# Index scores moved between the products of two projection panels, the key norm taken sooner, and two of four token tiles scaled by ScalarE before their transposition

## The chip, the cores and the metric

The kernel runs on one NeuronCore of a Trainium2 chip, as one launch. The metric is device time in microseconds. Before the change it was 1379.87 us, the median of three runs (1375.46 to 1380.01).

## What is computed

Two transformer blocks over 512 tokens of width 1024, in fp32. The first has windowed attention with sinks beside differential attention, then a feed-forward part with a short convolution. The second, `hybrid_layer`, has sparse latent attention whose keys are chosen by an index, beside a recurrent branch. The parts that the change touches:

```python
def rms_norm(x, g):        # also at the ends of the first block's two halves
    xf = xf * lax.rsqrt(jnp.mean(xf * xf, axis=-1, keepdims=True) + EPS)
    return (xf * g.astype(jnp.float32)).astype(x.dtype)
...
        x = x + rms_norm(jnp.einsum("bse,ed->bsd", mix, w_out[layer]), attn_post_g[layer])
        h2 = rms_norm(x, ffn_pre_g[layer])
        f = conv_ffn(h2, w_up[layer], conv_w[layer], conv_b[layer], w_down[layer])
        x = x + rms_norm(f, ffn_post_g[layer])
...
    z = xn @ w_in
    q, c_kv, q_idx, k_idx, w_idx, g_attn, x_rnn, g_rnn, merge = split_cols(z)
    c_kv = rms_norm_2(c_kv, kv_norm_g)
    k_idx = layer_norm(k_idx, idx_ln_g, idx_ln_b)
...
        s_idx = jax.nn.relu(jnp.einsum('btjd,bsd->btjs', qi.astype(f32), k_idx_f))
        s_idx = jnp.einsum('btjs,btj->bts', s_idx, wi.astype(f32))
        s_idx = jnp.where(causal[None], s_idx, -jnp.inf)
        _, idx = lax.top_k(s_idx, topk)
```

There are 8 index heads of width 64, and each query keeps 128 keys.

## The kernel before

**Products.** An fp32 product is made of three fp32r products, of a rounded high part and a low rest: high by high, high by low, low by high. Weights come as 100 panels of 256 columns by 1024 rows, loaded by SyncE's queue into two raw buffers. ScalarE makes the high part (`hi`, L850), VectorE (`lo`, L1296) or GpSimd (L332) the low part; each feeds the panel two further on. `one_panel` (L339) multiplies a panel: 16 passes, each of three matmuls of 512 columns, the first 8 passes for the first half of the panel's columns, the others for the second. It starts once its low part stands (`w_lo`) and the panel two before it has been copied out of PSUM (`evac`). PG holds the two panels in work, PX the side products.

**Token-wise norms, n2 and n4.** The last two panels of the stages out1 and dn3 leave their result with tokens on the partitions, in four tiles t of 128 tokens (Y4 and F4). Per tile, VectorE adds the last half (L1537, L1663), ScalarE squares it with a sum (`half_squares`, L891) and takes a root (L906), and VectorE makes 1 over the root with one Newton step and a diagonal matrix DG from it (`token_factor`, L1520 to L1525). TensorE multiplies each 128x128 piece of the tile with DG (L440), which scales and transposes at once: `turn_all` runs the chunks 0 to 5, the tiles 0 and 1 first, then tile 2, then tile 3; `turn_rest` the chunks 6 and 7 inside the next panel. VectorE then updates the residual (L1549) and ScalarE and VectorE split it (L923, L1554) for the first panel of the next stage, up0 or in2a. VectorE does tile t wholly before it adds tile t+1.

**Norms n3 and n5.** The sum of squares over the 1024 rows is one product with a constant matrix in `mean_square` (L390), two fp32 matmuls, issued between panel 0 and panel 1 of up0 and of in2a. They wait until VectorE has added the squares (L1273). From the sum ScalarE makes R by a logarithm and an exponential, and no panel of the stage is copied out before R stands.

**in2a and the index.** in2a has seven panels: 0 the latent and the index key, 1 and 2 the index queries QI, 3 to 6 the attention queries. Side products (the index weights w_idx, the means and sums of the latent and the key) stand after panels 1 to 4. ScalarE and VectorE split the queries and the normed key into high and low (QIH, QIL, KIH, KIL), the last of these after panel 6. Then, between in2a and the next stage xr, a loop of 24 units runs alone: unit u is head u % 8 of query block u // 8 + 1, three fp32r matmuls with 64 rows and n = 256, 384 or 512 columns (L725 to L727), into one of four PG banks. ScalarE takes the positive part (L1125, two buffers RLU), VectorE adds it times the head's weight into MD (L1726). Unit u waits for ScalarE's unit u-4, ScalarE's unit u for VectorE's unit u-2, and xr for ScalarE's last.

**Top-k.** 16 rounds of `topk_round` (L1741, L1744) on VectorE follow: 3, 2, 1 and 2 in the four panels of xr, 1 at the end of rg, 3, 2 and 2 in wr. The result is needed only after wr.

## Time and profile before

| | |
|---|---|
| time, median of three | 1379.87 us |
| the profiled execution's own time | 1380.44 us |
| its span, first to last instruction | 1378.3 us |
| busy: PE, VectorE, ScalarE, GpSimd | 96%, 62%, 42%, 16% of the span |
| mean granted TensorE clock | 0.983 of 2.4 GHz |

PE is TensorE's matmuls, which are pipelined: the time that one takes from the next is the distance between two starts, not the duration in the row. A wait is idle time of an engine just ahead of an instruction, with the instruction whose end closed it. The rows below come from one execution, so sums are made against 1380.44 us.

### The profile page before, as it was taken

The page shows a single profiled execution, that of the slowest core. Times are in us where ns is not written, and L with a number is a line of the kernel's source. Part 1 is how long each engine was busy: PE and PEld are TensorE (multiplying, and loading weights), DVE is VectorE, ACT ScalarE, POOL GpSimd, SP SyncE. Part 2 cuts the span into 40 slices and gives each one's busy share as a digit, 9 for nine tenths or more (in the row PEclk, how much of TensorE's full clock was granted, in tenths as well). Part 3 has the DMA queues.
Part 4 walks back from the last instruction along what each step waited for, and adds up shares of the span by engine and source line. Part 5 has one row for each costly group of instructions (what it writes and reads, how often), then busy time and mean ns, then how long its engine had stood idle before and what let it go on. Part 6 is the DMA issues. An engine that isn't in the chain of part 4 may idle for free.

```text
span 1378.3 us, 16092 instructions
## 1 busy us (share of the span) xinstructions
PE 1316.8 (96%) x5982; PEld 1032.8 (75%) x5982; DVE 854.3 (62%) x1497; ACT 579.6 (42%) x872; POOL 219.7 (16%) x173
## 2 busy tenths in 40 slices
PE   7999988899999999999999999999999989999996
PEld 6777656688888888888888867777778856658885
DVE  6455753798888378738863532568887656663342
ACT  5344645634443134324322444323673246653321
POOL 1322211000000000000000023420005411114450
PEclk9999998999999999999999999899999999999999
DMA  5211100132222223222232131402122210002411
GB/s 193 92 62 61 62 31 31 61 107 106 92 91 91 95 104 107 92 92 92 91 111 103 62 146 69 153 31 92 62 96 92 101 49 31 32 31 92 153 62 61
DMA packets 17788, 116.52 MB, mean 85 GB/s; under 512 B 1984, under 2 KB 2240, under 8 KB 4544
## 3 DMA queue, kind: packets, MB, share of 16 engines
q1 hardware_dynamic: 16320, 108.35, 22.2%
q10 hardware_dynamic: 1408, 7.37, 1.4%
q8 instruction: 38, 0.62, 0.2%
q14 instruction: 22, 0.18, 0.0%
HBM read 111.52 MB, written 4.19 MB: 84 GB/s over the span
## 4 chain that ended last, share of the span: by engine, by line
PE 85%; DVE 10%; ACT 3%; issue 1%; DMA 1%; DVEq 0%; ACTq 0%; SPq 0%
PE PG L352 17%; PE PG L354 17%; PE PG L353 17%; PE PX L494 5%; PE PX L763 3%; PE PX L430 2%; PE PX L428 2%; PE PX L429 2%; PE PG L430 2%; PE PG L428 2%; PE PG L429 2%; PE PG L792 2%; PE PX L671 1%; PE PX L802 1%; DVE MD L1726 1%
## 5 line engine op out<-in xcount | busy, mean ns | idle before, releaser
L352 PE MATMUL PG<-XH,WH 128*128 128x512 f32 x992 | 392.2, 395 | 5.9 <-DVE XL L1554 2.7
L332 POOL TENSOR_TENSOR WL<-RAW,WH 128x512 fp32r<-128x512 f32 x160 | 216.5, 1384 | 1126.0 <-ACT WH L850 1126.0
L354 PE MATMUL PG<-XH,WL 128*128 128x512 f32 x992 | 387.1, 390 | 0.0
L353 PE MATMUL PG<-XL,WH 128*128 128x512 f32 x992 | 387.0, 390 | 0.0
L850 ACT ACTIVATE WH<-RAW 128x2048 fp32r<-128x2048 f32 x100 | 191.5, 1915 | 382.9 <-PE PG L354 270.7
L352 PEld LDWEIGHTS PG<-XH,WH 128*128 128x128 f32 x992 | 186.8, 188 | 47.9 <-issue 8.0
L353 PEld LDWEIGHTS PG<-XL,WH 128*128 128x128 f32 x992 | 186.9, 188 | 40.1 <-issue 2.1
L354 PEld LDWEIGHTS PG<-XH,WL 128*128 128x128 f32 x992 | 186.6, 188 | 39.0
L1296 DVE TENSOR_TENSOR WL<-RAW,WH 128x2048 fp32r<-128x2048 f32 x60 | 137.3, 2288 | 52.2 <-ACT WH L850 52.0
L1052 ACT ACTIVATE Z<-Z 128x512 f32<-128x512 f32 x32 | 20.2, 633 | 164.7 <-DVE Z L1605 164.7
L1589 DVE TENSOR_TENSOR U<-PG,R 128x1024 f32<-128x1024 f32 x32 | 39.2, 1224 | 53.2 <-PE PG L354 48.5
L354 PE MATMUL PG<-RH,WL 128*128 128x512 f32 x128 | 49.9, 390 | 0.0
L430 PE MATMUL PX<-WL,AH 128*128 128x512 f32 x128 | 49.9, 390 | 0.0
L428 PE MATMUL PX<-WH,AH 128*128 128x512 f32 x128 | 49.9, 390 | 0.0
L430 PE MATMUL PG<-WL,AH 128*128 128x512 f32 x128 | 49.9, 390 | 0.0
L428 PE MATMUL PG<-WH,AH 128*128 128x512 f32 x128 | 49.9, 390 | 0.0
L429 PE MATMUL PG<-WH,AL 128*128 128x512 f32 x128 | 49.9, 389 | 0.0
L429 PE MATMUL PX<-WH,AL 128*128 128x512 f32 x128 | 49.9, 389 | 0.0
L352 PE MATMUL PG<-RH,WH 128*128 128x512 f32 x128 | 49.8, 389 | 0.0
L1040 ACT ACTIVATE C<-U,COL 128x512 f32<-128x512 f32 x64 | 48.2, 800 | 0.1
L1600 DVE SCALAR_TENSOR_TENSOR C<-U,COL,C 128x510 f32<-128x510 f32 x64 | 45.1, 747 | 3.7
L980 ACT ACTIVATE PTM<-PX 128x128 f32<-128x128 f32 (+3 forms) x64 | 24.5, 435 | 49.7 <-PE PX L671 49.7
(309 smaller groups left out, 2086.6 us busy)
## 6 DMA issues: line engine op xcount, KB each, us to landing
RAW<-panels SPq DMA_DIRECT2D x100, 1024.0 KB, 4.7
x_spill<-XT ACTq DMA_DIRECT2D x1, 2048.0 KB, 7.1
XT<-x_spill ACTq DMA_DIRECT2D x1, 2048.0 KB, 7.7
outT<-SQ SPq DMA_DIRECT2D x4, 512.0 KB, 3.0
XT<-xT ACTq DMA_DIRECT2D x2, 512.0 KB, 6.4
XT<-xT SPq DMA_DIRECT2D x2, 512.0 KB, 9.1
RGW<-rgw ACTq DMA_DIRECT2D x1, 1024.0 KB, 4.7
UK<-uk ACTq DMA_DIRECT2D x1, 512.0 KB, 5.7
```

Of the source, the lines that this page charges most:

```text
L332: ins = pool.tensor_tensor(WL[:, s].rearrange("p a b -> p (a b)")[:, piece], RAW[:, s, piece], WH[:, s].rearrange("p a b -> p (a b)")[:, p ...
L352: pe.matmul(o, WH[:, s, c, ms], xh[:, c, :], start=(c == 0), stop=False)
L353: pe.matmul(o, WH[:, s, c, ms], xl[:, c, :], start=False, stop=False)
L354: mm = pe.matmul(o, WL[:, s, c, ms], xh[:, c, :], start=False, stop=(c == DC - 1))
L428: pe.matmul(o, ah, wh, start=(half == 0 and c == 0), stop=False)
L429: pe.matmul(o, al, wh, start=False, stop=False)
L430: mm = pe.matmul(o, ah, wl, start=False, stop=(half == 1 and c == 3))
L494: mm = pe.matmul(PX[:, 2, :], w[:, s, c, m * P:(m + 1) * P], x[:, c, :], start=(c == 0 and w is WH and x is XH), stop=(c == DC - 1 and w i ...
L850: act.activation(WH[:, s].rearrange("p a b -> p (a b)"), RAW[:, s, :], ACT.Copy).then_inc(w_hi, 1)
L1040: ins = act.activation(C[:, b, m, :], U[:, b, m, :], ACT.Identity, bias=col("cb", k + 32 * m), scale=col("cw2", k + 32 * m))
L1296: dve.tensor_tensor(WL[:, s].rearrange("p a b -> p (a b)"), RAW[:, s, :], WH[:, s].rearrange("p a b -> p (a b)").bitcast(F32), ALU.subtrac ...
L1600: step_(dve.scalar_tensor_tensor(out=C[:, b, m, 2:], in0=U[:, b, m, 0:S - 2], scalar=col("cw0", n + 32 * m), in1=C[:, b, m, 2:], op0=ALU.m ...
```

## The change

- The loop of 24 units goes away. `one_panel` takes `between`, and after passes 4 to 15 of panel 3 and passes 2 to 13 of panel 4 of in2a it issues one unit each, into the four banks of PX. Unit 0 waits for the first query half and the key's two parts, unit 3 for the second query half.
- So that these stand in time, the side products follow panel 1 (sums, w_idx, key sums), the key and latent norms share one pair of table loads on ScalarE, and QIH and QIL are made in halves. ScalarE's high parts for the panels are put among these steps: that for panel 2 ahead of R, that for panel 4 behind the second half of QIH.
- VectorE adds the units before it copies out panels 3 and 4, does three top-k rounds ahead of the copy of panel 5 and three after panel 6, and then 3, 2, 1, 1 in xr, 1 in rg and 1, 1 in wr.
- n2 and n4: VectorE adds tile 1 and then 2 before the factors of tiles 0 and 1, and makes the low part of the next panel ahead of tile 0. For tiles 0 and 1 it makes a number per token, no DG; ScalarE scales the tile's 1024 columns in place by it, and TensorE only transposes. Tiles 2 and 3 keep DG.
- n3 and n5: `mean_square` is issued after four passes of panel 1, not before it (`quarter_done`).

```diff
+        IDX_PLACES = {3: {4 + n: n for n in range(12)}, 4: {2 + n: 12 + n for n in range(12)}}
...
-                mm.then_inc(panel_done, 1)
+                    if quarter_done is not None and (m, c) == (0, 3):
+                        quarter_done()
+                    if (m, c) == (1, DC - 1):
+                        mm.then_inc(panel_done, 1)
+                    if m * DC + c in between:
+                        idx_scores(between[m * DC + c])
...
+                sums = {0: lambda: mean_square(norm, [(acc, 1, src[:, 0, :]), (acc, 1, src[:, 1, :])])}
+                if chunk_done is None:
+                    gemm(name, ready=(once(ready), 0), after={**sums, **more})
+                else:
+                    gemm(name, ready=(once(ready), 0), after=more, chunk_done=chunk_done, quarter={1: sums[0]})
...
-                    mm = pe.matmul(o, src, DG[:, t, :], start=True, stop=True)
+                    if t < 2:
+                        mm = pe.transpose(o, src, IDN[:])
+                    else:
+                        mm = pe.matmul(o, src, DG[:, t, :], start=True, stop=True)
...
-                pe.wait_ge(once("tok_factor"), 4 * TURN[norm] + 2)
+                pe.wait_ge(once("tok_scaled"), 2 * TURN[norm] + 2)
...
-            gemm_norm("in2a", "n5", SQF, "x3_split", {1: w_idx, 2: kv_sums, 3: ln_sums, 4: turns},
-                      turn_rest("n4", F4, "x3_new"))
-            pe.wait_ge(once("idx_split"), 2)
-            pe.wait_ge(evac, FIRST["xr"][0])
-            for u in range(3 * IDX_HEADS):
+            def idx_scores(u):
                 qb, j = u // IDX_HEADS + 1, u % IDX_HEADS
                 n = (qb + 1) * P
                 rows = slice((j % 2) * HD, (j % 2) * HD + HD)
+                if u == 0:
+                    pe.wait_ge(once("idx_split"), 2)
+                if u == 3:
+                    pe.wait_ge(once("idx_split"), 3)
                 if u >= 4:
                     pe.wait_ge(once("idx_relu"), u - 3)
                 qh, ql = (q[rows, j // 2, qb * P:(qb + 1) * P] for q in (QIH, QIL))
-                pe.matmul(PG[:, u % 4, 0:n], qh, KIH[rows, 0:n], start=True, stop=False)
-                pe.matmul(PG[:, u % 4, 0:n], qh, KIL[rows, 0:n], start=False, stop=False)
-                pe.matmul(PG[:, u % 4, 0:n], ql, KIH[rows, 0:n], start=False, stop=True).then_inc(once("idx_s"), 1)
-            pe.wait_ge(once("idx_relu"), 24)
+                pe.matmul(PX[:, u % 4, 0:n], qh, KIH[rows, 0:n], start=True, stop=False)
+                pe.matmul(PX[:, u % 4, 0:n], qh, KIL[rows, 0:n], start=False, stop=False)
+                pe.matmul(PX[:, u % 4, 0:n], ql, KIH[rows, 0:n], start=False, stop=True).then_inc(once("idx_s"), 1)
+            p0 = FIRST["in2a"][0]
+            acc = once("n5_acc")
+            one_panel(p0, p0 % 2, ready=(once("x3_split"), 0), chunk_done=turn_rest("n4", F4, "x3_new"))
+            one_panel(p0 + 1, (p0 + 1) % 2,
+                      quarter_done=lambda: mean_square("n5", [(acc, 1, SQF[:, 0, :]), (acc, 1, SQF[:, 1, :])]))
+            kv_sums()
+            w_idx()
+            ln_sums()
+            one_panel(p0 + 2, p0 % 2)
+            turns()
+            for k in range(3, 7):
+                one_panel(p0 + k, (p0 + k) % 2, between=IDX_PLACES.get(k, {}))
...
+                    if 1 <= t < 3:
+                        act.wait_ge(once("tok_factor"), 4 * TURN[norm] + t)
+                        act.activation(y[:, t - 1, :], y[:, t - 1, :], ACT.Copy, scale=RTK[:, 3 * t - 1:3 * t])\
+                            .then_inc(once("tok_scaled"), 1)
...
+            p0 = FIRST["in2a"][0]
+            hi_ahead(p0)
...
+            act.wait_ge(evac, p0 + 1)
+            act.activation(CSQ[:, 0, :], CKV[:, 0, :], ACT.Square).then_inc(once("kv_sq"), 1)
+            hi_ahead(p0 + 1)
+            act.wait_ge(once("ln_x"), 1)
+            act.activation(CSQ[:, 1, :], KC[:], ACT.Square).then_inc(once("ln_sq"), 1)
+            act.wait_ge(evac, p0 + 2)
+            act.activation(QIH[:, 0:2, :], QI[:, 0:2, :], ACT.Copy).then_inc(once("qi_hi"), 1)
+            act.preload_act_table_set("natural_log")
+            for name, k, bank in (("kv", 0, 1), ("ln", 1, 2)):
+                act.wait_ge(once(name + "_sum"), 1)
+                step_(act.activation(CSQ[:, k, :], PX[:, bank, :], ACT.Ln, bias=EPST))
+            act.wait_ge(act_step, step_.n)
+            for name, k in (("ln", 1), ("kv", 0)):
+                act.activation(CSQ[:, k, :], CSQ[:, k, :], ACT.Exp, scale=-0.5).then_inc(once(name + "_r"), 1)
+            act.wait_ge(once("ki_done"), 1)
+            act.activation(KIH[:], CKV[:, 1, :], ACT.Copy).then_inc(once("ki_hi"), 1)
+            act.wait_ge(evac, p0 + 3)
+            act.activation(QIH[:, 2:4, :], QI[:, 2:4, :], ACT.Copy).then_inc(once("qi_hi"), 1)
+            hi_ahead(p0 + 2)
+            for k in range(3, 7):
+                for u in IDX_PLACES.get(k, {}).values():
+                    n = (u // 8 + 2) * P
+                    act.wait_ge(once("idx_s"), u + 1)
+                    if u >= 2:
+                        act.wait_ge(once("idx_acc"), u - 1)
+                    act.activation(RLU[:, u % 2, 0:n], PX[:, u % 4, 0:n], ACT.Relu).then_inc(once("idx_relu"), 1)
+                hi_ahead(p0 + k)
+                if k == 4:
+                    act.wait_ge(once("x3_split"), 8)
+                    act.wait_ge(spilled, 16)
+                    act.dma_start(RGW[:], rgw_in).then_inc(loaded_b2, 16)
+                    act.dma_start(UK[:], uk_in).then_inc(loaded_b2, 16)
+                    act.dma_start(UV[:], uv_in).then_inc(loaded_b2, 16)
...
             def token_factor(norm, t):
-                v, r = MSV[:, t:t + 1], [RTK[:, 3 * t + k:3 * t + k + 1] for k in range(3)]
+                r = [RTK[:, 3 * t + k:3 * t + k + 1] for k in range(3)]
+                if t == 0:
+                    dve.wait_ge(once("tok_half"), TURN[norm] + 1)
+                dve.wait_ge(once("tok_sum"), 8 * TURN[norm] + NB + t + 1)
+                step_(dve.scalar_tensor_tensor(out=r[2], in0=SSB[:, t:t + 1], scalar=1.0 / 1024, in1=MSV[:, t:t + 1],
+                                               op0=ALU.mult, op1=ALU.add))
                 dve.wait_ge(once("tok_root"), 4 * TURN[norm] + t + 1)
                 link(dve.reciprocal(r[0], MSR[:, t:t + 1]))
-                link(dve.scalar_tensor_tensor(out=v, in0=SSB[:, t:t + 1], scalar=1.0 / 1024, in1=v,
-                                              op0=ALU.mult, op1=ALU.add))
-                link(dve.scalar_tensor_tensor(out=r[1], in0=r[0], scalar=v, in1=r[0], op0=ALU.mult, op1=ALU.mult))
+                link(dve.scalar_tensor_tensor(out=r[1], in0=r[0], scalar=r[2], in1=r[0], op0=ALU.mult, op1=ALU.mult))
                 link(dve.tensor_scalar(r[1], r[1], -0.5, 1.5, ALU.mult, ALU.add))
-                dve.tensor_scalar(DG[:, t, :], IDN[:], r[0], r[1], ALU.mult, ALU.mult).then_inc(once("tok_factor"), 1)
+                if t < 2:
+                    dve.tensor_tensor(r[2], r[0], r[1], ALU.mult).then_inc(once("tok_factor"), 1)
+                else:
+                    dve.tensor_scalar(DG[:, t, :], IDN[:], r[0], r[1], ALU.mult, ALU.mult).then_inc(once("tok_factor"), 1)
...
+            lo_ahead(p)
...
-                if t == 0:
+                if t == 1:
                     first_half("n2")
-                    lo_ahead(p)
-                token_factor("n2", t)
+                if t in (1, 2):
+                    token_factor("n2", t - 1)
+            token_factor("n2", 2)
+            token_factor("n2", 3)
...
+            in2a_out(0, CKV[:])
+            dve.wait_ge(once("wi_hi"), 1)
+            dve.tensor_tensor(WIL[:], WIR[:], WIH[:].bitcast(F32), ALU.subtract).then_inc(once("wi_split"), 1)
+            in2a_out(1, two(QI, 0))
+            dve.wait_ge(once("ln_mean"), 1)
+            dve.wait_ge(evac, p0 + 1)
+            dve.scalar_tensor_tensor(out=KC[:], in0=PX[:, 3, :], scalar=-1.0, in1=CKV[:, 1, :],
+                                     op0=ALU.mult, op1=ALU.add).then_inc(once("ln_x"), 1)
+            dve.wait_ge(once("qi_hi"), 1)
+            dve.wait_ge(evac, p0 + 2)
+            dve.tensor_tensor(QIL[:, 0:2, :], QI[:, 0:2, :], QIH[:, 0:2, :].bitcast(F32), ALU.subtract)\
+                .then_inc(once("idx_split"), 1)
+            dve.wait_ge(once("wx_ready"), 1)
+            dve.scalar_tensor_tensor(out=WXT[0:8, :], in0=PX[0:8, 0, :], scalar=IDX_HEADS ** -0.5 * HD ** -0.5,
+                                     in1=R[0:8, :], op0=ALU.mult, op1=ALU.mult).then_inc(once("wxt"), 1)
+            dve.wait_ge(once("ln_r"), 1)
+            dve.wait_ge(once("ln_x"), 1)
+            link(dve.scalar_tensor_tensor(out=KC[:], in0=KC[:], scalar=col("ln_g", 0), in1=CSQ[:, 1, :],
+                                          op0=ALU.mult, op1=ALU.mult))
+            dve.tensor_scalar(CKV[:, 1, :], KC[:], col("ln_b", 0), None, ALU.add).then_inc(once("ki_done"), 1)
+            dve.wait_ge(once("kv_r"), 1)
+            dve.scalar_tensor_tensor(out=CKV[:, 0, :], in0=CKV[:, 0, :], scalar=col("kv_norm", 0), in1=CSQ[:, 0, :],
+                                     op0=ALU.mult, op1=ALU.mult).then_inc(once("kv_done"), 1)
+            dve.wait_ge(once("ki_hi"), 1)
+            dve.wait_ge(once("ki_done"), 1)
+            dve.tensor_tensor(KIL[:], CKV[:, 1, :], KIH[:].bitcast(F32), ALU.subtract).then_inc(once("idx_split"), 1)
+            in2a_out(2, two(QI, 1))
+            dve.wait_ge(once("wx_turned"), 1)
+            link(dve.tensor_scalar(WX, PX[:, 3, 0:32], 1.0, None, ALU.mult))
+            dve.wait_ge(once("qi_hi"), 2)
+            dve.wait_ge(evac, p0 + 3)
+            dve.tensor_tensor(QIL[:, 2:4, :], QI[:, 2:4, :], QIH[:, 2:4, :].bitcast(F32), ALU.subtract)\
+                .then_inc(once("idx_split"), 1)
+            for t in range(3, 7):
+                for u in IDX_PLACES.get(t, {}).values():
+                    idx_add(u)
+                if t == 5:
+                    for _ in range(3):
+                        topk_round()
+                in2a_out(t, two(QT, t - 3))
+            for _ in range(3):
+                topk_round()
...
-                for _ in range(1 if t == 2 else 2 + (t == 0)):
+                for _ in range((3, 2, 1, 1)[t]):
...
-                for _ in range((3, 2, 2, 0)[t]):
+                for _ in range((1, 1, 0, 0)[t]):
```

## Rows read from the trace of the kernel before

**Rows 1.** The page, part 4: shares of the span in the chain that ended last

```profile
PE 85%; DVE 10%; ACT 3%; issue 1%; DMA 1%; DVEq 0%; ACTq 0%; SPq 0%
```

**Rows 2.** TensorE's waits: line and releaser, us in total, times, longest

```profile
PE PX L440 <- DVE DG L1525: 3.0, 4, 1.4
...
PE PX L390 <- DVE SQF L1273: 1.6, 1, 1.6
...
PE PG L352 <- DVE WL L1296: 0.7, 1, 0.7
```

**Rows 3.** Timeline, ScalarE, at panel ends: start, duration, instruction, [idle before]

```profile
879.48 1.91 ACT L850 ACTIVATE WH<-RAW 128x2048 fp32r<-128x2048 f32 x1 [8.44 <-PE PG L354]
...
913.92 1.92 ACT L850 ACTIVATE WH<-RAW 128x2048 fp32r<-128x2048 f32 x1 [12.95 <-PE PG L354]
...
924.80 1.92 ACT L850 ACTIVATE WH<-RAW 128x2048 fp32r<-128x2048 f32 x1 [8.96 <-PE PG L354]
```

**Rows 4.** Timeline, TensorE, inside the loop of index units

```profile
881.65 0.29 PE L726 MATMUL PG<-KIL,QIH 64*128 64x256 f32 x2
...
881.77 0.28 PE L727 MATMUL PG<-KIH,QIL 64*128 64x256 f32 x2
...
897.62 0.40 PE L726 MATMUL PG<-KIL,QIH 64*128 64x512 f32 x1
...
897.86 0.40 PE L727 MATMUL PG<-KIH,QIL 64*128 64x512 f32 x1
```

**Rows 5.** Windows: busy PE, PEld, DVE, ACT, POOL (count), granted clock, DMA share, GB/s

```profile
890.00:893.00 3.00, 3.00 (x14) 2.73 (x13) 2.86 (x5) 1.95 (x5) 0.00 (x0) 0.50 0.43 183
...
901.30:904.40 3.10, 3.10 (x7) 2.47 (x8) 0.55 (x1) 0.00 (x0) 0.00 (x0) 0.50 0.03 5
...
1160.00:1200.00 40.00, 38.84 (x216) 23.89 (x215) 25.38 (x86) 23.84 (x67) 5.23 (x4) 1.00 0.07 27
```

**Rows 6.** Timeline, TensorE, in the latent attention

```profile
1157.99 0.40 PE L763 MATMUL PX<-XH,WL 128*128 128x512 f32 x1
...
1158.32 0.70 PE L792 MATMUL PG<-KT,QT 64*128 64x256 f32 x4
...
1158.95 1.09 PE L671 MATMUL PX<-IDN,PM 128*128 128x128 f32 x8
```

**Rows 7.** The adds by tile (ns min/median/max), then GpSimd and top-k in the timeline

```profile
L1726 DVE SCALAR_TENSOR_TENSOR MD<-RLU,SM,MD x24: 484/619/1374, 882.6 to 901.1; 128x256 f32<-128x256 f32 x8, 128x384 f32<-128x384 f32 x8, 128x512 f32<-128x512 f32 x8
...
881.47 5.58 POOL L332 TENSOR_TENSOR WL<-RAW,WH 128x512 fp32r<-128x512 f32 x4 [5.84 <-ACT WH L850]
...
915.13 1.47 DVE L1741 MAX8 SM<-MD 128x8 f32<-128x256 f32 x3
```

**Rows 8.** Timeline, TensorE, around turn_all of n2 and of n4

```profile
242.68 0.39 PE L510 MATMUL PG<-WL,XH 128*128 128x512 f32 x1
...
250.26 0.49 PE L440 MATMUL PX<-DG,Y 128*128 128x128 f32 x2 [0.40 <-DVE DG L1525]
...
780.99 3.11 PE L440 MATMUL PX<-DG,F 128*128 128x128 f32 x24
...
785.84 0.38 PE L440 MATMUL PX<-DG,F 128*128 128x128 f32 x1 [0.40 <-DVE DG L1525]
```

**Rows 9.** Timeline, steps of a tile: VectorE, ScalarE, and squares of 1024 columns

```profile
249.02 0.16 DVE L1520 RECIPROCAL SM<-SM 128x1 f32<-128x1 f32 x1 [1.12 <-ACT SM L906]
...
249.86 0.35 DVE L1525 TENSOR_SCALAR DG<-IDN,SM 128x128 f32<-128x128 f32 x1
...
247.94 0.63 ACT L891 ACTIVATE SQY<-Y 128x512 f32<-128x512 f32 x1 [1.85 <-DVE Y L1537]
...
796.59 3.89 ACT L912 ACTIVATE SQF<-XT 128x1024 f32<-128x1024 f32 x4
```

**Rows 10.** Timeline, up0: the sum of squares, and the low part for panel 2

```profile
267.79 1.99 PE L390 MATMUL PX<-SQY,O 128*128 128x512 f32 x4 [1.57 <-DVE SQY L1273]
...
274.29 2.29 DVE L1296 TENSOR_TENSOR WL<-RAW,WH 128x2048 fp32r<-128x2048 f32 x1 [0.58 <-ACT WH L850]
```

More of the change, by code:

```diff
@@ L1656, in down_last @@
                     lo((p0 + k) % 2, p0 + k + 3)
+                lo_ahead(p0 + 2)
                 for t in range(NB):
@@ L1717, in _, with idx_add @@
             OFF = {1: 0, 2: 256, 3: 640}
-            for u in range(24):
+            def idx_add(u):
                 qb, j = u // 8 + 1, u % 8
```

90 lines of the change are left out of this document (15 added, 75 removed).

## The prediction, made before the changed kernel was run

> **What bounds the kernel now.** I read the shares of the chain that ended last first: TensorE's matmuls carry 85% of it [rows 1], so a change pays where TensorE stands still, runs at a low clock, or does work that can go. Next, TensorE's waits [rows 2]: 3.0 us for the diagonal matrices of the token-wise norms, 1.6 us for the added squares of n5 (n3 has a second wait like it, [rows 10]), and 0.7 us for one low part in rg. Last, the stretch between in2a and xr, where the index units run alone. ScalarE starts the next high part right when a panel ends, so the starts of L850 are panel ends: 924.80 - 913.92 = 10.88 us is one panel of xr at full clock, and 913.92 - 879.48 = 34.44 us lie between the end of in2a and the end of the first panel of xr [rows 3]. The stage thus costs 34.44 - 10.88 = 23.56 us. It is that dear because the units go at the pace of the round through ScalarE and VectorE, and since the granted clock is 0.50, the 1.2 GHz level, for most of it and for 3.1 us of xr [rows 5]. The first units still ran at full clock, 0.12 us apart [rows 4]; what TensorE did before it fell was to wait between units for ScalarE.
>
> **Part 1, the index units between passes.** Removed: 23.56 us. Added to panels 3 and 4: 24 units of three matmuls. At full clock one starts 0.12 us after the other at 256 columns and 0.24 us after it at 512 [rows 4]; for 384 I take the middle, 0.18. That is 3 x 8 x (0.12 + 0.18 + 0.24) = 13.0 us. What the trace doesn't show is a 64-row fp32r matmul between 128-row ones. The nearest row is in the latent attention: a 64-row matmul starts 0.33 us after a 128-row one, where the pitch is 10.88 / 48 = 0.23, so 0.10 us for a change of kind [rows 6]. A unit has two changes. Inside the loop a new unit cost nothing where nothing was waited for, and the latent attention's are fp32, not fp32r; so 0 to 4.8 us, and I take the middle, 2.4. Nothing below 0: no row shows a matmul that starts sooner than the one before it lets it. Part 1 gains 23.56 - 13.0 - 2.4 = **8.2 us**, between 5.8 and 10.6.
>
> The Trainium skill ("TensorE: Matmul & The Clock Gate", "Step-by-step: what each phase is for") says that TensorE pulls a weight load ahead of running matmuls if the row groups don't conflict or it goes to the background buffer. By that rule the changes would cost nothing and the sum would be 2.4 us lower; the row shows 0.10 us at such a change, and the middle stands.
>
> For that the units must not stall TensorE, which now has the rest of a panel behind each. Unit u waits for ScalarE's unit u-4 and so for VectorE's unit u-6. TensorE's pace is a pass, 0.68 us, and a unit: 1.0 us at 256 columns, 1.4 at 512. VectorE needs 0.48 to 0.8 us for an add, but 1.37 at most while GpSimd makes a low part [rows 7]. That work takes 5.6 us a panel, so some four adds come at 1.4 us, together 1.5 us behind TensorE; the ring gives six units, over 5 us. Free. Also queued behind each other now:
> - On ScalarE the high part for panel 4 starts behind the second half of QIH, so 2.2 us after panel 2's end, not at it (the copy of the panel, 1024 columns, about half of a low part's 2.29 [rows 10]; half of QIH, half of L850's 1.92 [rows 3]). With 1.9 us for itself and 5.6 (GpSimd) it stands 10 us after that end, while panel 3 with 12 units lasts over 16. Free.
> - The positive parts stand behind that high part: it ends 4.1 us after panel 2's end, and unit 0 comes after five passes, 3.4 us, plus its own 0.4. Free.
> - Key and query halves: w_idx (24 matmuls at 0.23) and three sums (0.9 each, half of the pair in [rows 10]) keep TensorE until 8 us past panel 1's end; the key's logarithm and two exponentials, two VectorE steps, KIH and KIL are seven operations of 512 columns at 0.6 to 0.7, with a table load and handoffs some 7 us, and panel 2 lasts 10.88. Unit 0 finds them done. Unit 3 needs QIL's second half, some 3.5 us past panel 2's end; it comes at 6.5.
> - VectorE does three top-k rounds ahead of copying panel 5 out. A round is twice the three searches' 1.47 us and waits, 3.2 us [rows 7], so 9.7 us after the copy of panel 4, about when panel 5 ends. The copy is needed a panel later. Free.
> - The DMAs of RGW, UK and UV now go out on ScalarE's queue after panel 4, earlier, with nothing else on that queue; SyncE's order is untouched.
>
> **Part 2, n2 and n4.** Let E be the end of TensorE's last product. The tile 3 group of matmuls, on which the chain hangs, starts at 250.26, that is E + 7.35 with E = 242.68 + 0.23, in n2; and at E + 4.85 in n4, 785.84 after 780.99 [rows 8]. The difference is that n2 begins its tile steps late. Now the add of tile 3 ends at E + 0.8; the factor of tile 2 takes 249.86 + 0.35 - 249.02 = 1.2 us [rows 9], E + 2.0, that of tile 3 E + 3.2. TensorE has, from E + 2.0 on, four matmuls of tile 2 and, for chunks 4 and 5, four transposes and two matmuls. A DG matmul is two records, a transpose one (8 for 8 in [rows 6]), each 0.12 us (24 in 3.11 us, [rows 8]): 16 records, 1.9 us. Tile 3 starts at E + 3.9: 3.4 us sooner in n2 and 0.9 in n4. In `turn_rest` two of four matmuls a chunk become transposes, 2 x 2 x 0.12 = 0.5 us in each norm, on TensorE's path, as it is slower there than VectorE's chunk. Together **5.3 us**. The cover for the new work: ScalarE has per tile 249.02 - 247.94 = 1.1 us from the squares to the root's handover, and now 3.89 / 4 = 0.97 us for scaling [rows 9], 2.1 against 12 x 0.23 = 2.7 us in which TensorE makes a tile. The low part moved ahead of tile 0 (2.3 us) finds its high part ready in both. If ScalarE falls a tile behind, 2.1 us are lost in each, and the two together gain 5.3 - 4.2 = 1.1 us. If TensorE doesn't bind, tile 3 starts at E + 3.2: 6.7 us.
>
> **Part 3, the sums of squares.** TensorE stands 1.6 us in n3 and in n5, both for VectorE's last addition [rows 2, 10]. Four passes, 2.7 us, are put ahead of the two matmuls, which cost the same inside the panel: **3.2 us** gained. The sum starts 1.1 us later, and so does all that needs R. What is late next is the low part for panel 2 of up0: it ended at 274.29 + 2.29 = 276.6, 8.8 us after the sum's start at 267.79 [rows 10]. Now the sum starts 2.7 us into panel 1, the low part ends at 11.5, and panel 1 with the sum lasts 10.88 + 1.8 = 12.7. Covered by 1.2 us; without cover up to 1 us is lost, in up0 alone, as in2a's low part is made ahead of R.
>
> **Part 4, top-k.** The one wait of rg for a low part on VectorE, 0.7 us [rows 2], should go, as VectorE enters rg one round, 3.2 us, sooner: **0.7 us**. The five rounds fewer in wr give nothing, since TensorE doesn't wait there.
>
> **Sum.** 8.2 + 5.3 + 3.2 + 0.7 = 17.4 us. 1380.44 - 17.4 = 1363.0 for the profiled execution, which stands 0.6 us above the median; against that, 1379.87 - 17.4 = **1362.5 us**. The bounds of the terms: gain 5.8 + 1.1 + 2.2 + 0 = 9.1 at worst, 10.6 + 6.7 + 3.2 + 0.7 = 21.2 at best, times from 1358.7 to 1370.8.
>
> **Rivals.**
> - *The round binds, not TensorE.* VectorE's adds stay slow beyond GpSimd's work, or the steps ahead of unit 0 come late, and TensorE waits inside panels 3 and 4. Against: the counts above. For: the round was what the loop waited for. If all 24 units went at 1.4 us plus the pass's rest, that is 0.4 us more for the 8 shortest and 0.1 to 0.2 for the rest, 6 us are lost: 1368.5 us. Chance 0.12.
> - *ScalarE is late at the norms.* The scaling keeps the squares of tile 3 from starting, and the gain of part 2 falls to 1.1 us: 1366.7 us. For: three things now hang on ScalarE within one tile. Chance 0.10.
> - *The clock falls in panels 3 and 4; slower.* From 890 to 893 us TensorE was busy throughout with 64-row matmuls and the clock stayed at 0.50, while 128-row ones brought it back within 3.1 us [rows 5]. It decides if the level falls to 1.2 GHz while units lie between the passes, likeliest in panel 4, where a unit takes as long as a pass. Both panels hold 2 x 12 passes of 0.68 us within their mixed parts and 15.4 us of units, 31.7 us, which would take as much again: 1362.5 + 31.7 = 1394 us; panel 4 alone, some 17 us, would end at 1379.5. Against: in the latent attention, where 64-row matmuls lie between 128-row ones, the clock was 1.00 over 40 us [rows 5]. Chance 0.04 for both panels, 0.03 for panel 4 alone.
>
> **How the numbers follow.** The forecast with its bounds has 0.71. Over 0.5% faster means under 1373.0, which the forecast and the first two rivals give: 0.93. Within 0.5%, about what a measurement of this kernel can tell from no change, is one panel at the low clock: 0.03. Slower is both panels: 0.04. The range takes in the first two rivals and nearly the whole of the bounds, with 1 us below the best for what a run scatters: 1357.5 to 1370.0, which leaves out the low clock and a corner.
>
> **What would show it.** In the profile of the changed kernel: no stretch between panel 6 of in2a and xr; panel 3 some 6 to 7 us and panel 4 some 9 us longer than 10.88; granted clock 1.00 throughout in2a; waits on RLU near nothing; the first DG matmul of tile 3 at E + 3.9 in both norms; no wait of L390's matmuls. It would be wrong if TensorE waits inside panels 3 or 4, if the clock drops there, or if TensorE idles at E for the scaled tiles by more than half a microsecond.

## The result, and the profile after

The changed kernel takes 1372.11 us (median of 9 runs, 1367.59 to 1373.32), the kernel before 1378.12 us (9 runs, 1375.30 to 1384.44) on the same chip. The ratio is 0.9947 (95%: 0.9930 to 0.9965): 0.5% faster. Predicted were 1.3%, 1362.5 us, and a time between 1357.5 and 1370.0 us. The profiled execution took 1372.33 us, its span is 1370.2 us.

To see where the gain stands at each point, take the starts of ScalarE's high part, which follow the ends of panels (L850 before, as in [rows 3], L876 after), in the two profiles:

| point | before | after | ahead | won since the row above | predicted |
|---|---|---|---|---|---|
| out1 begins | 232.21 | 231.07 | 1.14 | 1.1 | 0 |
| up0, panel 3 on (behind n2, n3) | 313.45 | 306.37 | 7.08 | 5.9 | 5.5 |
| in2a, first panels (behind n4, n5) | 816.31 | 805.85 | 10.46 | 3.4 | 3.0 |
| first panel of xr done (behind the index) | 913.92 | 902.17 | 11.75 | 1.3 | 8.2 |
| latent attention begins (behind rg) | 1092.01 | 1079.16 | 12.85 | 1.1 | 0.7 |
| latent attention ends | 1239.21 | 1231.02 | 8.19 | -4.7 | 0 |

Two rows are off: the index stage gained 1.3 us and not 8.2, and the latent attention, which the change doesn't touch, gave back 4.7 us.

The page of the changed kernel, part 4, shares of the span in the chain that ended last (before: [rows 1]):

```profile
PE 93%; DVE 4%; ACT 1%; issue 1%; DMA 0%; DVEq 0%; ACTq 0%; SPq 0%
```

VectorE's part of the chain went from 10% to 4% and TensorE's rose from 85% to 93%: the loop that went at VectorE's pace is gone, but the path runs through TensorE's matmuls in its place. TensorE's waits in the changed kernel (line and releaser, us in total, times, longest):

```profile
PE PX L685 <- DVE PM L1946: 12.3, 5, 4.6
...
PE PX L454 <- DVE DG L1566: 1.0, 2, 0.5
...
PE PX L452 <- ACT Y L936: 0.2, 1, 0.2
PE PX L452 <- ACT F L936: 0.2, 1, 0.2
```

The waits on DG fell from 3.0 us to 1.0, those on the added squares and on the low part [rows 2] are no longer in the list, and the scaled tiles cost 0.2 us in each norm. No matmul of in2a's passes waits for RLU. The largest entry, 12.3 us in the latent attention, was there before the change as well, with 11.3 us; the 1.0 us between them is one of its stalls, the third large one (see the experiments on the clock).

Now a unit between two passes. Timeline of TensorE in the changed kernel (start, duration, instruction):

```profile
828.18 0.39 PE L356 MATMUL PG<-XL,WH 128*128 128x512 f32 x1
828.41 0.39 PE L357 MATMUL PG<-XH,WL 128*128 128x512 f32 x1
828.73 0.38 PE L739 MATMUL PX<-KIH,QIH 64*128 64x256 f32 x1
828.95 0.28 PE L740 MATMUL PX<-KIL,QIH 64*128 64x256 f32 x1
829.07 0.27 PE L741 MATMUL PX<-KIH,QIL 64*128 64x256 f32 x1
829.27 0.50 PE L355 MATMUL PG<-XH,WH 128*128 128x512 f32 x1
829.61 0.40 PE L356 MATMUL PG<-XL,WH 128*128 128x512 f32 x1
829.84 0.39 PE L357 MATMUL PG<-XH,WL 128*128 128x512 f32 x1
```

Read the distances of the starts. Within a pass it is 0.23 us, between two 64-row products of 256 columns 0.12, as in the loop before [rows 4]. But from L357 to the unit's first product it is 0.32 (0.09 too much), from that to the second 0.22 (0.10), from the third to L355 0.20 (0.08), and from L355 to L356 0.34 (0.11). There are four dear distances and not two, 0.09 + 0.10 + 0.08 + 0.11 = 0.38 us, about 0.4 us for each unit, and none is a wait. The pitch of pass and unit stays so for the wider ones:

```profile
841.87 0.44 PE L739 MATMUL PX<-KIH,QIH 64*128 64x384 f32 x1
...
843.47 0.44 PE L739 MATMUL PX<-KIH,QIH 64*128 64x384 f32 x1
...
858.05 0.50 PE L739 MATMUL PX<-KIH,QIH 64*128 64x512 f32 x1
...
859.83 0.49 PE L739 MATMUL PX<-KIH,QIH 64*128 64x512 f32 x1
```

1.60 us with 384 columns and 1.78 with 512, 1.44 with 256; less 0.68 for the pass, a unit costs 0.76, 0.92 and 1.10 us. 8 x (0.76 + 0.92 + 1.10) = 22.2 us, where 13.0 + 2.4 had been put into the sum, and 23.56 us went. The clock is not in it, nor a wait. The window over panels 3 and 4 (busy time of PE, PEld, DVE, ACT, POOL with counts, granted clock, DMA share, GB/s):

```profile
815.00:870.00 55.00, 55.00 (x219) 35.83 (x218) 25.61 (x36) 19.71 (x32) 11.21 (x8) 1.00 0.17 58
```

In the latent attention the granted clock falls to its lower level, 1.2 GHz, behind the first of TensorE's stalls on PM (its waits for the softmax product PM) and behind three later ones. Windows of the changed kernel behind the four, each with a stretch at 0.50 and the rest at 1.00:

```profile
1100.00:1106.00 6.00, 5.19 (x17) 3.25 (x18) 3.27 (x12) 1.87 (x7) 0.67 (x1) 0.72 0.52 175
1141.00:1147.00 6.00, 5.70 (x27) 4.67 (x28) 3.17 (x11) 2.23 (x7) 0.03 (x1) 0.72 0.48 175
1175.00:1181.00 6.00, 5.21 (x24) 4.43 (x24) 3.40 (x10) 2.23 (x7) 0.52 (x1) 0.72 0.50 175
1210.00:1216.00 6.00, 5.70 (x28) 4.83 (x29) 3.25 (x11) 2.23 (x7) 0.03 (x1) 0.72 0.47 175
```

6.00 x (1 - 0.72) = 1.7 us of full clock are lost in each. In the kernel before, only the first stall had a low stretch behind it (below, with its second profile).

### The profile page after: what moved, and what is told of

Same layout as the page of the kernel before. It is cut to its first block, busy times and chain, and to the rows that moved or that the text cites. A ratio compares the mean times of both kernels' runs of the same rounds, so it can differ in the third digit from the quotient of the medians.

```text
span 1370.2 us, 16031 instructions
## 1 busy us (share of the span) xinstructions
PE 1319.3 (96%) x5950; PEld 1026.7 (75%) x5950; DVE 853.3 (62%) x1498; ACT 581.2 (42%) x875; POOL 218.9 (16%) x173
## 3 DMA queue, kind: packets, MB, share of 16 engines
HBM read 111.52 MB, written 4.19 MB: 84 GB/s over the span
## 4 chain that ended last, share of the span: by engine, by line
PE 93%; DVE 4%; ACT 1%; issue 1%; DMA 0%; DVEq 0%; ACTq 0%; SPq 0%
PE PG L355 19%; PE PG L357 19%; PE PG L356 19%; PE PX L508 5%; PE PX L789 3%; PE PG L441 2%; PE PX L441 2%; PE PG L440 2%; PE PX L440 2%; PE PG L439 2%; PE PX L439 2%; PE PX L685 2%; PE PG L818 2%; PE PX L828 1%; PE PX L522 1%; PE PX L626 1%
## 5 line engine op out<-in xcount | busy, mean ns | idle before, releaser
L355 PE MATMUL PG<-XH,WH 128*128 128x512 f32 x992 | 392.9, 396 | 2.7 <-DVE XL L1598 2.7
L335 POOL TENSOR_TENSOR WL<-RAW,WH 128x512 fp32r<-128x512 f32 x160 | 215.6, 1378 | 1118.8 <-ACT WH L876 1118.8
L356 PE MATMUL PG<-XL,WH 128*128 128x512 f32 x992 | 386.2, 389 | 0.0
L357 PE MATMUL PG<-XH,WL 128*128 128x512 f32 x992 | 386.2, 389 | 0.0
L876 ACT ACTIVATE WH<-RAW 128x2048 fp32r<-128x2048 f32 x100 | 191.5, 1915 | 354.4 <-PE PG L357 244.2
L355 PEld LDWEIGHTS PG<-XH,WH 128*128 128x128 f32 x992 | 186.2, 188 | 48.7 <-issue 10.0
L356 PEld LDWEIGHTS PG<-XL,WH 128*128 128x128 f32 x992 | 186.3, 188 | 39.2 <-issue 1.9
L357 PEld LDWEIGHTS PG<-XH,WL 128*128 128x128 f32 x992 | 186.2, 188 | 38.9
L355 PE MATMUL PG<-RH,WH 128*128 128x512 f32 x128 | 49.8, 389 | 0.0
L357 PE MATMUL PG<-RH,WL 128*128 128x512 f32 x128 | 49.8, 389 | 0.0
```

What stands on the lines that cost most here:

```text
L335: ins = pool.tensor_tensor(WL[:, s].rearrange("p a b -> p (a b)")[:, piece], RAW[:, s, piece], WH[:, s].rearrange("p a b -> p (a b)")[:, p ...
L355: pe.matmul(o, WH[:, s, c, ms], xh[:, c, :], start=(c == 0), stop=False)
L356: pe.matmul(o, WH[:, s, c, ms], xl[:, c, :], start=False, stop=False)
L357: mm = pe.matmul(o, WL[:, s, c, ms], xh[:, c, :], start=False, stop=(c == DC - 1))
L876: act.activation(WH[:, s].rearrange("p a b -> p (a b)"), RAW[:, s, :], ACT.Copy).then_inc(w_hi, 1)
```

## The experiments

### What a unit costs

The changed kernel once more.

> The changed kernel once more, nothing edited. Its first profile shows the granted clock below 1.00 behind all four stalls of TensorE in the latent attention (the wait on the softmax product PM), where the kernel before shows it behind the first alone, and 4.7 us of the gain of 12.9 us that stood at its start are gone at its end. Theory A, the clock falls there in every execution of this kernel: the profile again shows a loss of 4 to 5 us between the start of the latent attention and its end, four stretches below 1.00, and a time of 1371 to 1373 us. Theory B, each stall has a chance to bring the clock down whatever the kernel: the count of low stretches and the loss differ from the first profile (0 to 3 us of loss, 1 to 3 stretches), and the time of a profiled execution lies 1 us lower for each stretch that is missing, down to 1367 us.

1372.48 us (1367.51 to 1373.49). Every point of the table above lies within 0.04 us of the first profile from up0 on, the four low stretches are there, and so is the loss of 4.7 us (12.84 us ahead, then 8.16). Theory B's chance in each execution is not what this profile shows. One run of the six took 1367.51 us at a mean clock of 0.990 where the others have 0.985 or 0.986. It has no profile, so in which stage it gained isn't known; the two profiles of the kernel before (below) differ by as much, ahead of out1.

Two units at a place:

```diff
-IDX_PLACES = {3: {4 + n: n for n in range(12)}, 4: {2 + n: 12 + n for n in range(12)}}
+IDX_PLACES = {3: {5 + 2 * n: (2 * n, 2 * n + 1) for n in range(6)},
+              4: {3 + 2 * n: (12 + 2 * n, 13 + 2 * n) for n in range(6)}}
```

> The same 24 units of index products, but two behind each other at 12 places between passes instead of one at each of 24 places. Theory, each trip from the passes into a unit and back costs 0.40 us at the joints whatever stands between: 12 trips fewer give 12 x 0.40 = 4.8 us, panels 3 and 4 of in2a end 4.8 us sooner, the time is 4.8 us below the changed kernel's. Rival, each unit costs its 0.40 us by itself (its first product and its 64-row operands), wherever it stands: no change, within 1 us.

1361.91 us (1359.89 to 1363.41), ratio to before 0.9874 (0.9853 to 0.9894). That is 10.2 us below the changed kernel where 4.8 were expected; the index stage (from in2a's first panels to xr, as in the table) won 24.68 - 12.61 = 12.1 us and not 1.3. The timeline says why:

```profile
851.16 0.39 PE L358 MATMUL PG<-XH,WL 128*128 128x512 f32 x1
851.48 0.50 PE L740 MATMUL PX<-KIH,QIH 64*128 64x512 f32 x2
851.81 0.40 PE L741 MATMUL PX<-KIL,QIH 64*128 64x512 f32 x2
852.05 0.40 PE L742 MATMUL PX<-KIH,QIL 64*128 64x512 f32 x2
852.37 0.50 PE L356 MATMUL PG<-XH,WH 128*128 128x512 f32 x1
852.71 0.39 PE L357 MATMUL PG<-XL,WH 128*128 128x512 f32 x1
```

The six products of two units stand in three rows of x2: the second unit's run at the same time as the first's. The pair costs 852.37 - 851.16 - 0.23 + 0.11 = 1.09 us, as much as one unit of 512 columns alone. Neither theory had that.

Four units at a place, at six places:

```diff
+IDX_PLACES = {3: {7 + 4 * n: tuple(range(4 * n, 4 * n + 4)) for n in range(3)},
+              4: {4 + 4 * n: tuple(range(12 + 4 * n, 16 + 4 * n)) for n in range(3)}}
```

> The 24 units in groups of four at 6 places. Theory of the joints: 18 trips fewer give 7.2 us less than the changed kernel. Rival, a cost of each unit: no change. Second rival, ScalarE and VectorE now bind: a unit of 512 columns takes ScalarE and VectorE longer than TensorE, so the next group would wait for a bank of PX; panel 4 has a wait on idx_relu in its profile, and the gain is 3 us or less.

1358.81 us (1354.95 to 1359.72), ratio 0.9843 (0.9821 to 0.9865): 13.3 us below the changed kernel where 7.2 were expected. The index stage won 14.6 us. By trips and pairs: a trip costs 0.4 us, and two units cost the bare columns of one, (22.2 - 24 x 0.4) / 2 = 6.3 us in all. So 12 trips come to 11.1 us and 6 to 8.7, which is 11.1 and 13.5 us less than 22.2; measured, against the changed kernel's stage: 10.8 and 13.3. ScalarE and VectorE don't bind: TensorE has no wait on RLU.

Products over all 128 rows, which leaves out the choice of the head, so the scores are other numbers:

```diff
-                rows = slice((j % 2) * HD, (j % 2) * HD + HD)
+                rows = slice(0, P)
```

> The index products contract over all 128 rows (both heads of a pair) instead of the 64 of their own head, so the index scores are other numbers; columns and count of products are the same. Theory, the 0.40 us at the joints belong to the change between products of 64 and of 128 rows: each unit costs its bare columns, 24 x 0.40 = 9.6 us less than the changed kernel, first products at 0.22 us or less behind the pass. Rival, the joints cost the same between any products of other columns or another bank: no change, 0.32, 0.22, 0.12, 0.20, 0.34 us as before within 0.02.

1360.16 us (1357.47 to 1362.71), ratio 0.9852 (0.9826 to 0.9879). The index stage won 10.8 us, 9.5 more than in the changed kernel (expected 9.6). Timeline:

```profile
846.01 0.40 PE L357 MATMUL PG<-XH,WL 128*128 128x512 f32 x1
846.25 0.33 PE L739 MATMUL PX<-KIH,QIH 128*128 128x384 f32 x1
846.41 0.34 PE L740 MATMUL PX<-KIL,QIH 128*128 128x384 f32 x1
846.59 0.35 PE L741 MATMUL PX<-KIH,QIL 128*128 128x384 f32 x1
846.78 0.40 PE L355 MATMUL PG<-XH,WH 128*128 128x512 f32 x1
```

0.24, 0.16, 0.18, 0.19, and 0.23 to the next matmul of the pass: the dear distances are gone, though bank, columns and engines are the same. The joint belongs to the change between 64 and 128 rows, and the rival (a joint between any products of other columns or another bank) falls.

The pairs again, with the heads in an order in which the two units of a pair read the same 64 rows (VectorE's `idx_add` has the same order):

```diff
-                qb, j = u // IDX_HEADS + 1, u % IDX_HEADS
+                qb, j = u // IDX_HEADS + 1, (0, 2, 1, 3, 4, 6, 5, 7)[u % IDX_HEADS]
```

> The kernel with the units in pairs, but the heads in the order 0, 2, 1, 3, 4, 6, 5, 7, so that the two units of a pair read the same 64 rows (0 to 63, or 64 to 127) and not one half each. Columns, places and joints are the same. Theory, the two units of a pair ran beside each other in the two halves of the rows (a pair of 512 columns took 1.09 us over its pass, a single unit 1.10 us), so a pair on the same rows takes its second unit on top: 4 x 0.36 + 4 x 0.53 + 4 x 0.70 = 6.4 us more than the pairs before (1361.9 us), 1368 to 1369 us, panels 3 and 4 longer by 6 to 7 us. Rival, the second unit of a pair is cheap for another reason (it needs no joint of its own and its weights are loaded ahead): no change, within 1 us of 1361.9 us.

1365.55 us (1361.03 to 1368.83), ratio 0.9883 (0.9841 to 0.9924). The time was expected at 1368 to 1369 us. The four times lie 7.8 us apart, so they don't decide between the theories; the stage in the profile does: it won 17.32 - 11.42 = 5.9 us, 6.2 us less than the pairs of both halves (expected 6.4). The products stand one by one again:

```profile
854.34 0.50 PE L740 MATMUL PX<-KIH,QIH 64*128 64x512 f32 x1
854.67 0.39 PE L741 MATMUL PX<-KIL,QIH 64*128 64x512 f32 x1
854.91 0.39 PE L742 MATMUL PX<-KIH,QIL 64*128 64x512 f32 x1
855.14 0.39 PE L740 MATMUL PX<-KIH,QIH 64*128 64x512 f32 x1
```

Two units run beside each other only if each has its own half of the rows, and next to each other in the order. Placed singly between passes, no unit has such a neighbour.

### The parts one by one

The norms n2 and n4 alone (`turn_back`, `turn_all`, the tile steps of ScalarE, `token_factor` and its order).

> The kernel before with one part of the change: tiles 0 and 1 of n2 and n4 scaled by ScalarE and turned with the identity, with VectorE's new order of factors. Theory, as in the prediction: 3.9 us at n2 and 1.4 us at n4, 5.3 us together, none of it lost on the way to the index loop. Rival, the gain of 5.9 us seen in the changed kernel by the first panel of up0 belongs in part to the mean square moved in n3 (1.6 us of it): then n2 alone gives 4.3 us. Second question, the clock in the latent attention. Theory A (it falls behind all four stalls only in the changed kernel): here one stretch below 1.00, as in the kernel before, and the gain stays at the end. Theory B (chance, or when the stall comes): one to four stretches, each costing about 1.7 us.

1379.2 us (1374.62 to 1381.46), ratio 0.9993 (0.9976 to 1.0009): nothing left. The gain is made nonetheless: by the starts of the high part 3.6 us at n2 (0.55 to 4.19 us ahead) and 1.1 at n4 (4.20 to 5.27), against 3.9 and 1.4. Then 0.7 us go in the index loop and 4.1 in the latent attention, where the profile has four low stretches.

The sums of squares alone (`gemm_norm` with the matmuls of the sum behind the fourth pass of panel 1).

> The kernel before with one part of the change: the matmuls of the mean square of n3 and n5 moved from behind the first panel to the first quarter of the second. Theory, as in the prediction: the wait of 1.57 us on the squares goes in both norms, 3.2 us together (1.6 at up0, 1.6 at in2a), and nothing takes its place. Rival, the matmuls now wait for something else behind the first quarter and only part is won: 1 to 2 us together. In the latent attention: as for the run of the norms, one low stretch by theory A, one to four by theory B.

1376.34 us (1371.81 to 1376.96), ratio 0.9974 (0.9959 to 0.9989). 1.8 us at n3 and 1.9 at n5, 3.7 us together (3.2 expected). In the latent attention nothing is lost: the kernel is 5.03 us ahead at its start and 5.10 at its end, 1.35 of which it had before out1.

The index part alone.

> The kernel before with the index part of the change alone (with it the norms of the keys sooner, and the mean square of n5 moved). Theory of the joints: the units cost 22.3 us between the passes of panels 3 and 4, where the loop before cost 24 us from its first product to xr, so by the first pass of xr 1 to 2 us are won from the units, 1.6 us from the mean square of n5, and 0.7 to 1.1 us in rg: 3.5 to 4.5 us ahead of the latent attention. Theory B for the clock: 0 to 5 us of that are lost in the latent attention, by the number of low stretches (one in the kernel before, four in the changed one), so the time is 1375 to 1378 us. Rival, the norms and the mean squares set the end of in2a in another way and this part alone gives 8 us.

1379.78 us (1375.08 to 1380.30), ratio 1.0003 (0.9988 to 1.0018). 1.8 us at n5, 1.3 from the units, 1.1 in rg, 4.99 us ahead of the kernel before at the latent attention (0.80 of it before out1); 4.3 of them go there, again with four low stretches, and the time ends above the 1375 to 1378 us expected. So neither the index part nor the norms is at the root of that loss, as each has it alone.

### The clock in the latent attention

The kernel before, a second profile.

> The kernel before once more, nothing edited, for a second profile of its latent attention. Theory A (the changed kernel brings the clock down there, the kernel before does not): one low stretch again behind the first stall, 3.4 us of clock lost, none behind the stalls of 2.1 to 3.0 us. Theory B (whatever the kernel, by chance or by when the stall comes): another number of low stretches, up to four, and a time of 1375 to 1385 us that goes with the number of them.

1375.0 us. Windows behind the four stalls:

```profile
1107.00:1114.00 7.00, 5.89 (x16) 3.35 (x17) 3.44 (x10) 1.70 (x6) 0.97 (x1) 0.51 0.45 152
1149.00:1155.00 6.00, 5.32 (x35) 4.35 (x36) 4.70 (x18) 2.71 (x8) 0.41 (x1) 1.00 0.48 178
1181.00:1187.00 6.00, 5.38 (x36) 4.38 (x37) 5.24 (x18) 3.81 (x13) 1.70 (x2) 1.00 0.51 175
1214.00:1220.00 6.00, 5.51 (x36) 4.50 (x37) 4.59 (x18) 2.89 (x9) 0.22 (x1) 1.00 0.49 175
```

As in the first profile: 3.4 us of clock lost at the first stall, none later. This execution was 5.4 us shorter than the first, but all of that, 5.57 us, stands ahead of out1, where the granted clock lost 3.4 us in place of 8.5 over the first 240 us. So executions of one kernel do differ, but these two not in the latent attention. Three profiles (before twice, the sums alone) are so; in eight (the changed kernel twice, both kinds of pairs, groups of four, 128 rows, the norms and the index part alone) a low stretch follows each of the four stalls. Yet the second and the fourth stall are as long in both kinds. The second one in the kernel before and in the one with the norms alone (in brackets TensorE's idle time ahead of the row, and what ended it):

```profile
1149.68 0.88 PE L671 MATMUL PX<-IDN,PM 128*128 128x128 f32 x6 [2.11 <-DVE PM L1888]
```

```profile
1149.33 1.08 PE L674 MATMUL PX<-IDN,PM 128*128 128x128 f32 x4 [2.10 <-DVE PM L1907]
```

2.11 and 2.10 us, behind the same instructions; one was followed by full clock, the other by a low stretch. What differs is when the stall comes and what came before it. To test that, the changed kernel with work put ahead of the latent attention:

```diff
+            for _ in range(10):
+                pe.matmul(PX[:, 3, :], UK[:, 0:2, :].rearrange("p a b -> p (a b)"), CKV[:, 0, :], start=True, stop=True)
             mla_keys(0, 3)
```

> The changed kernel with ten products of 512 columns more (10 x 0.23 = 2.3 us of TensorE work whose result is written over) ahead of the latent attention; all from there on comes 2.3 us later. Theory, the stalls in the latent attention cost clock or not by when they come: in the kernel before (and in the run with the mean squares alone) the second, third and fourth stall cost none, in all others with part of the change each cost 1.7 us, and the later place is about that of the kernel before. So the extra work takes low stretches away: one stretch or two behind the first stall, none behind the others, 4.7 us less there, and the time is 2 us below the changed kernel although it does 2.3 us more. Rival A, the falls belong to the changed kernel's code and not to the time: four stretches again, 2.3 us slower. Rival B, chance in each execution: the median stays within 1 us of 2.3 us slower, with any count of stretches in the profile.

1379.36 us (1374.25 to 1381.91), ratio 0.9995 (0.9977 to 1.0012). The price was mistaken: these products are fp32, not fp32r, and ten of them put everything back by 16.94 - 8.39 = 8.55 us, not 2.3. With the place so moved, the windows behind the same four stalls are:

```profile
1104.00:1112.00 8.00, 6.72 (x19) 3.78 (x19) 4.41 (x15) 2.29 (x8) 1.14 (x1) 0.57 0.38 133
1146.00:1152.00 6.00, 5.16 (x35) 4.20 (x36) 4.70 (x18) 2.59 (x9) 0.57 (x1) 1.00 0.53 175
1179.00:1185.00 6.00, 5.27 (x35) 4.32 (x36) 4.70 (x18) 2.66 (x8) 0.45 (x1) 1.00 0.50 175
1212.00:1218.00 6.00, 5.39 (x25) 4.31 (x26) 3.22 (x10) 2.23 (x7) 0.34 (x1) 0.72 0.50 175
```

3.4 us behind the first, none behind the second and third, 1.7 behind the fourth: a third pattern, with the changed kernel's code and the same stalls (12.3 us), and 2.6 us lost in the stage in place of 4.7. Rival A, that the falls belong to the code, falls.

The third stall needs a word of its own, as it is not the same in the kernel before. There and with the sums alone it took 1.16 and 1.15 us, in the other kernels with part of the change or all of it, GpSimd's work unchanged, 2.1. With the sums alone, and in this run:

```profile
1182.08 0.87 PE L677 MATMUL PX<-IDN,PM 128*128 128x128 f32 x6 [1.15 <-DVE PM L1894]
```

```profile
1179.73 0.88 PE L685 MATMUL PX<-IDN,PM 128*128 128x128 f32 x6 [2.11 <-DVE PM L1948]
```

A step of VectorE over two columns ahead of it took 0.17 us in the first and 1.15 in the second. The second was followed by full clock, so the longer stall is not an effect of the clock. Of the 4.7 us that the changed kernel loses, 1.0 is thus the longer third stall and 3.7 are clock. The windows give 6.8 us of clock lost for 3.4; 0.5 of the 3.4 fell inside the first stall and cost nothing, so the difference is 3.9, near the 3.7. The 2.6 us of this run are 1.0 of stall and 1.7 of clock.

The time missed the expectation (2 us below the changed kernel). The median came out 7.3 us above the changed kernel for 8.55 us of work, so rival B (chance in each execution) isn't shut out by the times, only by the profiles, which repeat within a kernel. That the place of a stall decides is thus argued, not shown: the added work also changed what TensorE did ahead of the first stall. What in the chip fixes when a stall counts was not settled.

### The stalls themselves

What holds TensorE there is VectorE, and VectorE is held by GpSimd. GpSimd and VectorE in the changed kernel at the second stall:

```profile
1135.92 5.11 POOL L335 TENSOR_TENSOR WL<-RAW,WH 128x512 fp32r<-128x512 f32 x4 [35.25 <-ACT WH L876]
1137.32 1.15 DVE L1937 TENSOR_TENSOR SM<-SM 128x2 f32<-128x2 f32 x1
1138.59 2.66 DVE L1946 TENSOR_SCALAR PM<-PM,SM 128x384 f32<-128x384 f32 x2
```

Two columns take 1.15 us beside GpSimd's four pieces of 1.28 us, and end at 1138.47, with GpSimd's second piece (1135.92 + 2 x 1.28 = 1138.48). So the pieces were taken apart:

```diff
                 for q in range(4):
+                    if 0 <= j < 4:          # j = p - FIRST["ga"][0] - 2
+                        u = 8 * j + ((2, 3, 6, 7) if j == 0 else (3, 5, 6, 7))[q]
+                        pool.wait_ge(once("mla_probs"), u - 1)
+                        pool.wait_ge(once("mla_s"), u + 1)
                     piece = slice(512 * q, 512 * q + 512)
```

> The changed kernel with GpSimd's low parts of four weight panels in the latent attention cut up in time: each of the four pieces of 1.28 us waits for a unit of the softmax of its own (its scores done and the products of two units earlier scaled), where before all four pieces ran behind each other. Theory, the stalls of TensorE there (12.3 us in five waits on PM) come from VectorE waiting for GpSimd's pieces (a scaling of two 384-column tiles takes 2.66 us beside them and 0.88 us without, for 512 columns; a maximum of two columns 1.15 us and 0.16 us): each stall falls from 2 to 3 us to under 1 us, the first from 4.6 to about 2 us, the low stretches behind the second to fourth go, and with 1.7 us for each the time falls by 8 to 12 us below the changed kernel. Rival A, the stalls are of the softmax chain itself and stay: no change. Rival B, the pieces collide with VectorE at more places now and each costs a wait of 1 us: 2 to 4 us gained at most, or lost.

1356.32 us (1355.95 to 1358.44), ratio 0.9836 (0.9815 to 0.9857): 15.8 us below the changed kernel, where 8 to 12 were expected. TensorE's waits in the stretch, the scaling that ends the first stall with the piece that now waits for it, and the two steps of VectorE from the second stall, now without a piece beside them:

```profile
PE PX L690 <- DVE PM L1951: 2.6, 2, 2.2
```

```profile
1096.91 0.48 DVE L1951 TENSOR_SCALAR PM<-PM,SM 128x128 f32<-128x128 f32 x2
...
1097.45 0.69 PE L690 MATMUL PX<-IDN,PM 128*128 128x128 f32 x2 [2.16 <-DVE PM L1951]
1097.53 1.28 POOL L340 TENSOR_TENSOR WL<-RAW,WH 128x512 fp32r<-128x512 f32 x1 [11.29 <-DVE PM L1951]
...
1133.70 0.16 DVE L1942 TENSOR_TENSOR SM<-SM 128x2 f32<-128x2 f32 x1
...
1133.97 0.75 DVE L1951 TENSOR_SCALAR PM<-PM,SM 128x384 f32<-128x384 f32 x2
```

12.3 us of waits are 2.6 now, the scaling that ends the first stall takes 0.48 us where it took 2.40, the two columns 0.16 for 1.15, and there is one low stretch. From start to end of the latent attention the kernel wins 23.83 - 13.74 = 10.1 us against the kernel before, where the changed kernel loses 4.7. The 14.8 us between them are the 9.7 us of waits and 5.1 us of clock (6.8 less 1.7).

Both edits together:

> Both edits that are expected to gain: the index units in groups of four and GpSimd's pieces spread over the latent attention. If the two are independent, the time is that of the groups of four (1358.8 us) less what spreading gives (8 to 12 us by the theory of the stalls): 1347 to 1351 us. If spreading gives nothing: 1358 to 1360 us.

1341.04 us (1338.12 to 1342.68), ratio 0.9716 (0.9694 to 0.9739), 31.1 us below the changed kernel and below the 1347 to 1351 us expected, the shortest time measured here. The two edits add up (13.3 + 15.8 = 29.1) and 2.0 us more: in the latent attention the clock is at 1.00 throughout, the last low stretch is gone too, and the stage wins 11.3 us against the kernel before in place of 10.1.

## Why the prediction was wrong

- **Bound.** Right: TensorE bounds, and the stage between in2a and xr went at the pace of the round.
- **Part 1, the units.** The step that failed is the price of a change of kind. The row in the latent attention gave 0.10 us at one matmul [rows 6]; two changes a unit made 0.2, and as the loop showed nothing of the sort, half of that was taken, 24 x 0.1 = 2.4 us, with 24 x 0.2 = 4.8 as the end. Measured: 22.2 - 13.0 = 9.2 us, 0.38 a unit, because each change is paid at two matmuls, the first of the new kind and the one behind it. The row was right; it was read one matmul long, and the way back to 128 rows wasn't looked for. The loop before has no change of kind at all, so it could not show the price. With 9.2 the term is 23.56 - 13.0 - 9.2 = 1.4 us; 1.3 were measured.
- **The round and the covers.** Right: no wait in panels 3 and 4, each matmul at its pitch, clock 1.00. The rivals on the round and on the clock there didn't come, nor did the one on ScalarE at the norms (0.2 us of waits in each). Panels 3 and 4 grew by 22.2 us together, not by 15 to 16.
- **Part 2, n2 and n4.** Right. The tile 3 group starts 3.78 us behind E in n2 and 3.85 in n4 (predicted 3.9). Alone the part gives 4.7 us (predicted 5.3).
- **Part 3, the sums.** Right in kind, 3.7 us alone for 3.2: the wait is gone from both norms.
- **Part 4.** 1.1 us for 0.7; the wait for the low part is gone. Where the other 0.4 come from wasn't looked for.
- **What the sum put at nothing.** The sum took it, without a reason given, that a stage which the change only moves keeps its time. The latent attention lost 4.7 us: the three later stalls, which cost no clock in the kernel before, were each followed by a stretch that cost 1.7 us, the first cost less clock than before, and the third stall grew by 1.0 us. The prediction weighed the clock only where the change puts work. Either miss alone would have left the time in the stated range: 1362.5 + 6.9 = 1369.4 us, and 1362.5 + 4.7 = 1367.2. All together, 17.4 - 6.9 (units) - 4.7 (latent attention) + 0.8 (norms and sums) + 0.4 (rg) + 1.1 (ahead of out1, not of the change) = 8.1 us, which is what the two profiles differ by.

The Trainium skill has a rule that bears on Part 1, on another page than the one the prediction weighed: "TensorEngine Tiling (Array Packing)", "Key Properties", says that changing the tiling mode, not just the tile, drains TensorE, and that different tiles can work in parallel. The runs agree with both: 0.4 us for a unit and back, nothing where all products have 128 rows, and two units of different halves in the time of one. That it is a drain, no trace here shows. What the prediction drew from its page, that the changes cost nothing, did not come out: they cost 9.2 us.

For the stalls, the Trainium skill ("SBUF — State Buffer", "Terms") has a port pair that VectorE and GpSimd hold in turn, exclusively, for a whole instruction. The trace agrees: 1.15 us for two columns beside pieces of 1.28, ending with one of them, and 0.16 alone.

## What to carry to other kernels

Moving products of 64 rows between products of 128 is paid per trip, not per product: group them, and let neighbours use different halves of the rows. When a row prices a transition, read on until the pitch is back to normal, and look for the way back too. A stall that costs no clock today can cost it once the work ahead of it has changed, so a gain made early may be gone later; take the stall away rather than count on its place.

## What the hardware showed that I had not expected

- A change between 64-row and 128-row fp32r matmuls costs 0.08 to 0.11 us at each of two matmuls, 0.4 us there and back.
- Two 64-row units of different halves ran fully beside each other (1.09 us for two, 1.10 for one).
- The same stall of 2.1 us, behind the same instructions, was followed by 1.2 GHz in some kernels and by 2.4 GHz in others; each low stretch lost 1.7 us, at the first stall 1.7, 3.4 or, in one kernel, 5.1.
- Letting GpSimd's four pieces start apart, each behind a point of VectorE's chain, took 9.7 us of TensorE's waits away without a piece being shorter.
- An fp32 product of 512 columns took TensorE 0.86 us (ten of them 8.55), an fp32r one 0.23.
